# Rotary partners fetched by DMAs between partitions, and expert weights loaded in quarters, in a two-layer hybrid decoder trunk

## What is computed

```python
z = rms_norm(x) @ w_in           # 3584 columns: za | bq bk bv | cq ck cv cg
a = causal_spatial_gating(gelu(za))              # 4 groups x 64
b = dilated_attention(bq, bk, bv)                # 8 heads x 64
c = silu(cg) * groupnorm(retention(rotary(cq), rotary(ck), cv))   # 4 heads x 64
x = x + concat(a, b, c) @ w_out
x = x + hier_moe(rms_norm(x))    # 16 experts of 1024 -> 512 -> 1024, two per token

def rotary(x, pos):              # half = 32
    x1, x2 = x[..., :half], x[..., half:]
    return concatenate([x1 * cos - x2 * sin, x1 * sin + x2 * cos], -1)
```

## Time and profile before

| | us |
|---|---|
| median of 3 runs | 701.98 (701.27 to 702.2) |
| the profiled execution, its own time | 701.2 |
| its span | 699.4 |
| PE busy in the span | 662.6 (95%) |
| DVE busy | 298.5 (43%) |
| ACT busy | 192.0 (27%) |
| 238.21 MB on SP's DMA queue, share of 16 engines | 84.2% |

### The profile page before, as it was taken

One profiled execution on the slowest core, in us unless ns is written; L12 is line 12 of the kernel. 1 busy time (PEld: TensorE's weight loads), 2 busy tenths in 40 slices (PEclk: granted clock), 3 DMA queues, 4 the chain that ended last, 5 costly groups with the idle time before them and its releaser, 6 DMA issues.

```text
span 699.4 us, 9145 instructions
## 1 busy us (share of the span) xinstructions
PE 662.6 (95%) x3442; PEld 380.2 (54%) x3442; DVE 298.5 (43%) x632; ACT 192.0 (27%) x342; POOL 16.2 (2%) x29
## 2 busy tenths in 40 slices
PE   6999999999999999997999999999999999999883
PEld 5878778653444444431388878784543353352331
DVE  4478986611232122121474888673221322121234
ACT  3457543421111110100154554342201111111102
POOL 3100000200000000000020000000000000000000
PEclk9999999999999999999999999999999999999998
DMA  9985049999999999999986330998999999999991
GB/s 339 327 291 186 1 189 423 379 412 408 423 420 420 423 420 421 422 421 421 402 291 235 126 121 31 396 422 330 424 419 422 422 420 421 420 422 420 422 408 63
DMA packets 46027, 240.96 MB, mean 345 GB/s; under 512 B 3457, under 2 KB 3649, under 8 KB 21281
## 3 DMA queue, kind: packets, MB, share of 16 engines
q1 hardware_dynamic: 44800, 238.21, 84.2%
q0 software_dynamic: 1040, 2.04, 1.2%
q10 hardware_dynamic: 144, 0.13, 0.1%
HBM read 239.32 MB, written 1.05 MB: 344 GB/s over the span
## 4 chain that ended last, share of the span: by engine, by line
PE 75%; DMA 22%; DVE 1%; issue 1%; ACT 1%; DVEq 0%; SPq 0%
PE psum L1086 23%; PE psum L765 22%; DMA up_w<-in_w_up 21%; PE psum L1119 10%; PE psum L785 4%; PE psum L1066 3%; PE psum L1027 2%; PE psum L745 1%; PE psum L991 1%; PE psum L932 1%; DMA x<-in_x 1%; PE psum L1100 1%; PE psum L844 1%; PE psum L801 1%; PE psum L820 0%
## 5 line engine op out<-in xcount | busy, mean ns | idle before, releaser
L1086 PE MATMUL psum<-up_w,xT 128*64 128x512 f32 x512 | 114.2, 594 | 9.8 <-DMA up_w<-in_w_up 9.8
L1119 PE MATMUL psum<-down_w,scores 128*64 128x512 f32 x512 | 113.5, 595 | 0.0
L765 PE MATMUL psum<-piece_hi,hT_part 128*128 128x512 f32 x320 | 100.1, 394 | 0.0
L1086 PEld LDWEIGHTS psum<-up_w,xT 128*64 128x64 f32 x512 | 36.9, 137 | 83.7 <-issue 64.5
L1119 PEld LDWEIGHTS psum<-down_w,scores 128*64 128x64 f32 x512 | 36.6, 137 | 63.9 <-issue 61.6
L765 PEld LDWEIGHTS psum<-piece_hi,hT_part 128*128 128x128 f32 x320 | 59.0, 188 | 13.2 <-issue 1.7
L1523 DVE TENSOR_TENSOR y_lo<-psum,y_hi 128x512 fp32r<-128x512 f32 x32 | 22.1, 691 | 101.9 <-ACT y_hi L701 101.9
L765 PE MATMUL psum<-piece_lo,hT_part 128*128 128x512 f32 x160 | 62.4, 390 | 0.0
L1086 PE MATMUL psum<-gate_a,xT 128*64 128x512 f32 x256 | 56.9, 594 | 5.0 <-DMA gate_a<-in_w_gate 5.0
L1086 PE MATMUL psum<-gate_b,xT 128*64 128x512 f32 x256 | 56.4, 593 | 0.0
L1502 DVE SCALAR_TENSOR_TENSOR work<-work,psum 128x512 f32<-128x512 f32 x16 | 11.0, 687 | 105.2 <-ACT work L690 105.2
(11 more groups left out here) (243 smaller groups left out, 834.0 us busy)
## 6 DMA issues: line engine op xcount, KB each, us to landing
up_w<-in_w_up SPq DMA_DIRECT2D x32, 2048.0 KB, 17.2
down_w<-in_w_down SPq DMA_DIRECT2D x64, 1024.0 KB, 14.4
gate_b<-in_w_gate SPq DMA_DIRECT2D x32, 1024.0 KB, 14.4
gate_a<-in_w_gate SPq DMA_DIRECT2D x32, 1024.0 KB, 18.3
up_w<-in_w_in SPq DMA_DIRECT2D x6, 2048.0 KB, 13.2
down_w<-in_w_in SPq DMA_DIRECT2D x4, 2048.0 KB, 20.7
down_w<-in_w_out SPq DMA_DIRECT2D x4, 2048.0 KB, 8.1
up_w<-in_w_in SPq DMA_DIRECT2D x4, 1024.0 KB, 8.8
```

The source lines that it names most:

```text
L765: ins = pe.matmul(o, tokens, w[b][:, c, :], start=(c == 0 and n == 0), stop=(c == DC - 1 and n == len(parts) - 1))
L1086: ins = pe.matmul(psum[e * SLOTS:(e + 1) * SLOTS, bank, :], xT[:, c, k:k + SLOTS], w[:, e, c, :], start=(c == 0), stop=(c == DC - 1))
L1119: ins = pe.matmul(psum[e * SLOTS:(e + 1) * SLOTS, 2 + n, :], heT[:, c, e * SLOTS:(e + 1) * SLOTS], down_w[:, e, c, n * COLS:(n + 1) * COLS ...
```

## The change

Two edits.

1. The permutation matrix and its two products go. SP issues, before the load of piece 7, four DMAs from `qkc` to `work1`, each moving 32 partitions of 4 KB to the neighbouring block of 32 partitions. It waits for them on `gelu_done` (a new count for the last read of `work1` by the GELU) and on `proj_copied_a` (the copy that makes `qkc`). DVE multiplies `work1` in place by a sine table whose sign now carries the minus.
2. `up_w` is always loaded in four quarters (1 MB for both experts, 4 KB in a row per partition and expert), and so is the one load of `gate_b` for pair 2. PE counts quarters in `gated` and `upped`, and waits for each quarter of `up_w`. The gate's `gate_loaded` still counts halves. The other gate loads and the down loads keep their halves.

```diff
-    put("sin", np.sin(ang.astype(np.float64)))
...
+    put("sin", np.sin(ang.astype(np.float64)) * np.where(i % HD < half, -1, 1)[:, None])
...
                     for b in halves:
                         if used is not None:
-                            sp.wait_ge(used.sem, used.at(g, b + 1 - back * used.turn))
+                            sp.wait_ge(used.sem, used.at(g, used.turn // 2 * (b + 1) - back * used.turn))
                             settle(sp)
-                        if dst is up_w:
-                            sp.dma_start(dst[:, :, 4 * b:4 * b + 4, :], src[bass.ds(q, 1), :, :, 4 * b:4 * b + 4, :]
-                                         .rearrange("q p e c n -> (q p) e c n")).then_inc(loaded[b].sem, 16)
-                            continue
...
+                def load_quarters(dst, src, arrived, used, g, q, back):
+
+                    for k in range(4):
+                        sp.wait_ge(used.sem, used.at(g, k + 1 - back * used.turn))
+                        settle(sp)
+                        sp.dma_start(dst[:, :, 2 * k:2 * k + 2, :], src[bass.ds(q, 1), :, :, 2 * k:2 * k + 2, :]
+                                     .rearrange("q p e c n -> (q p) e c n")).then_inc(arrived[k].sem, 16)
...
                 for n in range(2):
+                    if n == 1:
+
+                        sp.wait_ge(gelu_done.sem, gelu_done.at(l, 1))
+                        sp.wait_ge(proj_copied_a.sem, proj_copied_a.at(l, CQK))
+                        for k in range(4):
+                            there, here = slice((k ^ 1) * HD // 2, ((k ^ 1) + 1) * HD // 2), slice(k * HD // 2, (k + 1) * HD // 2)
+                            sp.dma_start(work1[there], qkc[here].rearrange("p c t -> p (c t)")).then_inc(swapped.sem, 16)
                     load_piece(6 + n, w_out_p[bass.ds(l, 1), :, :, n * COLS:(n + 1) * COLS]
                                .rearrange("l p c n -> (l p) c n"))
...
-                load_gate(first + 2, 0)
+                load_quarters(gate_w[0], gate_d, [gate_loaded[0][k // 2] for k in range(4)], gated, first + 2, pair(first + 2), 2)
                 load_up(first + 1)
...
                 project(BQ)
-                pe.wait_ge(const_loaded.sem, 16)
...
                     ins.then_inc(spatial_done.sem, 1)
-                    pe.wait_ge(proj_copied_a.sem, proj_copied_a.at(l, CQK))
-                    for n in range(2):
-                        ins = pe.matmul(psum[:, 2 + n, :], C("swap"), qkc[:, 2 * n:2 * n + 2, :].rearrange("p c t -> p (c t)"),
-                                        start=True, stop=True)
-                    ins.then_inc(swapped.sem, 1)
                     score(1)
...
-                            if c % 4 == 0:
-                                pe.wait_ge(loaded[c // 4].sem, loaded[c // 4].at(turn_of, loaded[0].turn))
+                            if c % per_load == 0:
+                                pe.wait_ge(loaded[c // per_load].sem, loaded[c // per_load].at(turn_of, loaded[0].turn))
...
-                            if c % 4 == 3:
+                            if c % 2 == 1:
                                 ins.then_inc(done.sem, 1)
...
                 partner = work1.rearrange("p (c t) -> p c t", c=4)
-                dve.wait_ge(swapped.sem, swapped.at(l, 1))
-                V.tensor_tensor(partner, psum[:, 2:4, :].rearrange("p b (c t) -> p (b c) t", c=2),
+                dve.wait_ge(swapped.sem, swapped.at(l, 4 * 16))
+                V.tensor_tensor(partner, partner,
                                 C("sin").unsqueeze(1).to_broadcast([P, 4, SEQ]), ALU.mult).then_inc(swap_read.sem, 1)
```

More of the change, by code:

```diff
@@ L54 @@
 GELU_CUBE = 0.044715
-CONST_PARTS = [("ident", P), ("ones", P), ("logc", 3 * P), ("decay", 4 * 2 * P), ("cos", SEQ), ("sin", SEQ), ("swap", P),
+CONST_PARTS = [("ident", P), ("ones", P), ("logc", 3 * P), ("decay", 4 * 2 * P), ("cos", SEQ), ("sin", SEQ),
                ("before", P), ("slot", SLOTS), ("index", EXPERTS), ("causal", P)]
@@ L285, in hybrid_trunk @@
         normed, attended, gated_c = signal("normed", 2), signal("attended", 2), signal("gated_c", 1)
-        swapped, swap_read, rotated = signal("swapped", 1), signal("swap_read", 1), signal("rotated", 1)
-        cos_done = signal("cos_done", 1)
+        swapped, swap_read, rotated = signal("swapped", 4 * 16), signal("swap_read", 1), signal("rotated", 1)
+        cos_done, gelu_done = signal("cos_done", 1), signal("gelu_done", 1)
         inner_ready, decayed = signal("inner_ready", 1), signal("decayed", 1)
@@ L307, in hybrid_trunk @@
         gate_loaded = [[signal(f"gate_loaded{o}{b}", 32) for b in range(2)] for o in range(2)]
-        up_loaded = [signal(f"up_loaded{b}", 16) for b in range(2)]
+        up_loaded = [signal(f"up_loaded{k}", 16) for k in range(4)]
         down_loaded = [signal(f"down_loaded{b}", 32) for b in range(2)]
-        gated, upped, gate_tanh = signal("gated", 2, 8), signal("upped", 2, 8), signal("gate_tanh", 1)
+        gated, upped, gate_tanh = signal("gated", 4, 8), signal("upped", 4, 8), signal("gate_tanh", 1)
         gate_open = signal("gate_open", 1)
@@ L316, in hybrid_trunk @@
         scattered, x_added = signal("scattered", 4), signal("x_added", 4, 3)
-        VSTEPS = 110
+        VSTEPS = 109
         v_step = signal("v_step", VSTEPS)
@@ L437, in _ @@
                 sp.wait_ge(projected.sem, projected.at(l, BV + 1))
-                load_halves(up_w, up_d, up_loaded, upped, first, l * PAIRS, 1)
+                load_quarters(up_w, up_d, up_loaded, upped, first, l * PAIRS, 1)
                 sp.wait_ge(attended.sem, attended.at(l, 2))
@@ L461, in load_up @@
                 def load_up(g):
-                    load_halves(up_w, up_d, up_loaded, upped, g, pair(g), 1)
+                    load_quarters(up_w, up_d, up_loaded, upped, g, pair(g), 1)
                 def load_down(g):
                     load_halves(down_w, down_d, down_loaded, downed, g, pair(g), 1)
-                load_gate(first + 2, 0)
+                load_quarters(gate_w[0], gate_d, [gate_loaded[0][k // 2] for k in range(4)], gated, first + 2, pair(first + 2), 2)
                 load_up(first + 1)
@@ L688, in item @@
                     act.wait_ge(pickT_ready.sem, pickT_ready.item(g0, i, 1))
-                    act.wait_ge(gated.sem, gated.item(g0, i, 2))
+                    act.wait_ge(gated.sem, gated.item(g0, i, 4))
                     act.activation(sig, psum[:, 0, :], ACT.Tanh, scale=slot_scales[:, i % 2, 0:1]).then_inc(gate_tanh.sem, 1)
@@ L888, in _, with spatial_score @@
                 turn_tokens(1, PIECE_BANK[CQK])
-                def swap_score():
+                def spatial_score():
                     pe.wait_ge(vn_ready.sem, vn_ready.at(l, 1))
@@ L895, in swap_score @@
                     ins.then_inc(spatial_done.sem, 1)
-                    pe.wait_ge(proj_copied_a.sem, proj_copied_a.at(l, CQK))
-                    for n in range(2):
-                        ins = pe.matmul(psum[:, 2 + n, :], C("swap"), qkc[:, 2 * n:2 * n + 2, :].rearrange("p c t -> p (c t)"),
-                                        start=True, stop=True)
-                    ins.then_inc(swapped.sem, 1)
                     score(1)
-                project(CVG, swap_score)
+                project(CVG, spatial_score)
                 pe.wait_ge(rotated.sem, rotated.at(l, 1))
@@ L1077, in item @@
                         tokens_ready(pe, g0, *GATHER_IN[i - 1], DC - 1)
-                    for bank, w, loaded, turn_of, done in ((0, gate_w[o], gate_loaded[o], halves, gated), (1, up_w, up_loaded, g0 + i, upped)):
+                    for bank, w, loaded, per_load, turn_of, done in ((0, gate_w[o], gate_loaded[o], 4, halves, gated),
+                                                                     (1, up_w, up_loaded, 2, g0 + i, upped)):
                         for c in range(DC):
@@ L1308, in _ @@
                 dve.wait_ge(gelu_tanh.sem, gelu_tanh.at(l, 1))
-                link(V.scalar_tensor_tensor(zf, work1[:], 1.0, zf, ALU.add, ALU.mult))
+                V.scalar_tensor_tensor(zf, work1[:], 1.0, zf, ALU.add, ALU.mult).then_inc(gelu_done.sem, 1)
+                dve.wait_ge(gelu_done.sem, gelu_done.at(l, 1))
                 split_lo(CVG, 0)
@@ L1503, in item @@
                     dve.wait_ge(gate_open.sem, gate_open.item(g0, i, 1))
-                    dve.wait_ge(upped.sem, upped.item(g0, i, 2))
+                    dve.wait_ge(upped.sem, upped.item(g0, i, 4))
                     V.scalar_tensor_tensor(he, sig, slot_scales[:, i % 2, 1:2], psum[:, 1, :], ALU.mult, ALU.mult).then_inc(he_ready.sem, 1)
```

## The result

The changed kernel takes **705.21 us** (median of 6, 704.75 to 706.09) against 702.11 for the kernel before on the same chip (6 runs): ratio 1.0047, interval 1.0037 to 1.0057. It is slower by about 3.1 us; 704.6 was forecast. The profiled execution took 705.06, with a span of 703.3.

A forecast was written before the change was run, and what follows sets the result against it. The experts' weight stream was taken to bound the kernel, each layer ending 3.46 us after its last byte. Terms +0.2 - 0.6 + 3.0 = +2.6 us gave 703.8 on the profiled execution and a forecast of 704.6, range 701.2 to 707.5.

The forecast's parts named there:

- Permutation products off PE: 0: Before score(1): the 1.72 us per layer of products only filled PE's wait for gated_a; at most 0.08 gained, counted 0.
- Four DMAs: 0: Partner transfers on SP: landing 2.5 us after issue, before DVE asks; w_out's second half 5.4 us later; cost 0.
- a transfer of 7 us: Late case of the partner DMAs: lateness over 0.2 us paid in both layers, +2.9, giving 707.5.
- Earlier release: Start of the experts: quarters issue 1.75 us earlier in layer 1, 0.6 kept; layer 0's 0.42 hole and part of 0.31 go.
- Smaller pieces: 0.25 us a load, +3.0: up_w stream: 4 KB rows cost 0.25 us a load, over six loads per layer (pairs 2 to 7) +3.0.
- Finer waits at the end: 0: End of a layer: last up quarter leaves 8 products, 1.84 us sooner, but PE then waits for down_w; saves nothing.
- Layer 0 against layer 1: Split of the loss: +0.2 early in layer 0, -0.6 in layer 1, then +3.0 from six up loads per layer.
- the filled holes: Stream gaps early in the experts: 0.42 and about half of 0.31 us gained in layer 0, 0.6 in layer 1.
- Free packets: Rival: 4 KB rows run at 421 GB/s, only the filled holes remain, 700.7 to 701.2; chance 0.20.
- dear packets: Rival: 4 KB rows cost up to the 2 KB price, 0.88 a load, up to 712, half way 707; chance 0.12.
- a shorter front: Rival: score(1) starts right behind L893, saving up to 1.72 us per layer; 701.2, or 698.5 with cheap packets; chance 0.08.
- a late partner: Rival: fourth partner DMA takes over 5.5 us and stalls DVE; +0.2 at the upper bound, 707.5 at 7 us; chance 0.08.

The follow-up runs named there:

- The first edit alone: Kernel before with only the rotary partners by four DMAs and the permutation products removed, all weights still in halves: 702.31 us, ratio 0.9996.
- the run with this part alone: Changed kernel with up_w back in halves of 2 MB DMAs, only pair 2's gate load in quarters, partners by DMA: 701.81 us, ratio 0.9999.
- gates_too: Changed kernel with the gate loads of pairs 3 to 7 also in quarters with 4 KB rows, ten more loads: 707.77 us, ratio 1.0082.
- 4 KB rows in halves: Kernel before with each half of up_w in two 1 MB DMAs of 4 KB rows, PE taking chunks in that order: 706.19 us, ratio 1.0065.
- the second edit alone: Kernel before with up_w and pair 2's gate load in quarters, permutation products kept on PE: 706.07 us, ratio 1.0058.
- gates_16kb: Kernel before with the gate loads of pairs 3 to 7 whole, in two 2 MB DMAs with 16 KB rows: 705.57 us, ratio 1.0046.
- gates_up_even_16kb: Kernel before with gates of pairs 3 to 7 and up_w of pairs 2, 4, 6 whole, in 16 KB rows: 701.65 us, ratio 0.9995.

## Why the prediction was right

- *What bounds the kernel.* Right. The stream of weights sets the end: kernels that differ only in the row length of up_w and in the order in which PE takes the chunks moved by 3.8 and 12.0 us, while PE's products stayed the same.
- *Permutation products off PE: 0.* Right, and to the number. Score(1) waits for DVE; 1.79 us of idle replaced 1.72 us of work. The first edit alone has the ratio 0.9996.
- *Four DMAs: 0.* Right. They land 2.4 us after issue (2.5 taken). SP needed 0.6 us for each, not 0.4, which the cover absorbed; w_out's second half went out 6.4 us later, not 5.4, which cost nothing either. The fixed part of about 2 us stands in the Trainium skill (DMA: Bandwidth & Descriptors, Anatomy of one DMA) for the path of GpSimd's DMAs, and these are SP's; the trace's 2.4 us is the number to use. The price of a transfer of 7 us was added up wrongly, 2.9 instead of 2 x 1.3 = 2.6; the upper end of the range would be 707.2 and not 707.5.
- *Earlier release.* Right in mechanism, too generous in size as far as can be told: SP issued 1.6 to 1.7 us earlier relative to PE, and the down load's release gave it back. I counted a gain of 0.6 in layer 1; the run with this part alone shows none beyond its interval of 0.7 us. The 4 KB rows without an earlier release cost 3.8 us (4.6 by the ratio) and the changed kernel 3.1 (3.3), which leaves room for a gain of 0.7 to 1.3, but the two intervals overlap.
- *Smaller pieces: 0.25 us a load, +3.0.* Right in mechanism, a little low. Measured are 0.27 (gates_too), and 0.32 by the medians or 0.38 by the ratio for 4 KB rows in halves (over 12 loads, though the loads ahead of the stretch are in it), each give or take about 0.1. The line through the 2 KB and 8 KB rates gave 0.29; shading it to 0.25 went the wrong way, though 0.25 lies within that error. The Trainium skill's 408.7 GB/s for a load stream with 4 KiB rows (DMA: Bandwidth & Descriptors, iDMA fabric) gives 0.30 as an estimate, and this case's 407 agrees.
- *Finer waits at the end: 0.* Right: 1.89 us of waiting for down_w instead of 0.3.
- *Layer 0 against layer 1.* I gave them +1.7 and +0.9; the profiles show +2.6 and +1.3. The +2.6 is just outside the 1.5 to 2.5 that I had named. Since kernels that should be equal differ by up to 1 us in layer 0, only the order is worth anything, and the second edit alone, with +2.2 and +2.4, doesn't repeat it.
- *Sum.* +2.6 forecast, +3.1 measured (2.6 to 4.0). With 0.29 for the 0.25 in all 15 loads the same sum gives +3.2. That it agrees so closely is partly luck, as the filled holes that I counted as gains, about 0.6 us in each layer, don't show in the time of any run.
- *Rivals.* Free packets are ruled out by the run with 4 KB rows in halves, dear packets by the same run (0.88 a load needs 2 KB rows, which measured 1.0), a shorter front by the first edit alone and by the first load of up_w at 95.62, a late partner by DVE's timeline.

## What to carry to other kernels

When a queue of weight loads sets the end, cutting a load finer helps only if the rows stay long: what counted here is the bytes in a row per partition, and not whether 2 MB come as one DMA or two. An earlier release or a finer wait is worth what the next event in the chain lets through, here nothing that could be measured; look for the load behind it before counting the gain. And before taking work off an engine, look whether it is only filling a wait.

## What the runs showed of the hardware

- The rate of the 16 DMA engines falls with the row length at the same size of DMA (1 MB for up_w): 422 GB/s for 8 KB, about 407 for 4 KB, 380 to 387 for 2 KB. With 16 KB rows, in DMAs of 2 MB, it is 427 to 430. All but the 422 are worked out from streams in which only a part of the bytes had such rows; the kernel before has 387 with 2 KB rows alone.
- SP's issue of a DMA can itself take long. In the changed kernel's chain of waits three single issues late in the stream take 4 to 8 us, two of up_w (L421, 4 KB rows) and one of down_w (L413, 8 KB rows), against some 0.4 to 0.6 at its start. The kernel before has it in a smaller measure: its two issues of up_w at 301.19 take 5.36 us, at 95.66 they take 0.88.

```profile
303.93 8.43 SPq L421
...
312.69 4.12 SPq L421
...
317.08 4.08 SPq L413
...
323.79 21.23 DMA down_w<-in_w_down
345.06 3.68 PE psum L1117 x16
```

  The last down load is issued at 323.79 and still has 21 us of queue in front of it, and the engines' share is 1.02 from 245 to 335, so I read it as costing nothing here; no run tests that, nor what the issue waits for.
- In gates_16kb, around a wait of 6.26 us, PE's granted clock was 0.57 in the window from 320 to 325 and 0.75 in the next, and 64 products took 1.8 to 2.0 us longer than at full clock. Shorter waits can do it too: in gates_up_even_16kb, after waits of 1.68 and 2.72 us with 32 gate products between them, it was 0.57 from 304 to 308, and 32 up products took 8.78 us, not 7.09. After 1.43 us in the same run it stayed 1.00.
